# Three query heads ahead of the expert rows, five among them

## The reference

```
qh = (t @ w_q).reshape(T, 8, 2, 128)                 # queries: two halves for each of 8 heads
s = einsum('thpd,hpnd->thpn', qh, sub_keys)          # key scores: 128 for each half
s_top, i_top = top_k(s, 16)                          # the best 16 of each half
cand = s_top[:, :, 0, :, None] + s_top[:, :, 1, None, :]
best, pos = top_k(cand.reshape(T, 8, 256), 16)       # the best 16 pairs: 16 experts for a head
g = softmax(best)
act = gelu(einsum('thkd,td->thk', u_tab[idx], t))
out = einsum('thk,thkd->td', g * act, v_tab[idx])
```

## Time and profile before

| | |
|---|---|
| median of 3 runs | 1783.69 us (1779.28 to 1784.22) |
| the profiled execution | 1787.91 us |
| its span | 1786.0 us |
| busy: PE, DVE, ACT, POOL | 87%, 58%, 43%, 15% |
| DMA | 431.63 MB, mean 242 GB/s |
| of these the gathers (queue 0) | 268.45 MB |
| chain that ended last, by engine | PE 59%, DMA 25%, ACT 7%, DVE 6% |

### The profile page before, as it was taken

How to read it: one execution, slowest core, us unless ns; L and a number is a source line. 1 busy time by engine, 2 the same in 40 slices (tenths; PEclk the granted TensorE clock), 3 DMA queues, 4 the chain that set the end, 5 groups by cost and what they waited for, 6 DMA issues and landing times.

```text
span 1786.0 us, 22981 instructions
## 1 busy us (share of the span) xinstructions
PE 1553.8 (87%) x8461; PEld 1127.9 (63%) x8461; DVE 1030.4 (58%) x2060; ACT 763.5 (43%) x1628; POOL 268.5 (15%) x260
## 2 busy tenths in 40 slices
PE   8899999978888877887777769988999988889997
PEld 5699559864233322322222239878999986889997
DVE  3345326435666666766666456544676676466665
ACT  2444333215444444444444343443555545454553
POOL 0000000104334444444444300000000000000000
PEclk9899999989999999999999999968999997899999
DMA  7355544487999999999999944402555541235552
GB/s 249 121 169 183 165 165 131 154 305 293 420 414 419 421 420 419 420 420 420 419 419 421 420 158 139 145 1 93 191 188 179 177 131 55 72 118 188 179 176 91
DMA packets 175284, 431.63 MB, mean 242 GB/s; under 512 B 6764, under 2 KB 133345, under 8 KB 142305
## 3 DMA queue, kind: packets, MB, share of 16 engines
q0 software_dynamic: 36864, 268.45, 36.4%
q1 hardware_dynamic: 137178, 159.51, 27.5%
q10 hardware_dynamic: 1159, 2.58, 0.4%
HBM read 429.47 MB, written 1.05 MB: 241 GB/s over the span
## 4 chain that ended last, share of the span: by engine, by line
PE 59%; DMA 25%; ACT 7%; DVE 6%; issue 2%; POOL 0%; ACTq 0%; DVEq 0%; SPq 0%; POOLq 0%
PE banks L577 27%; DMA arena<-in_peer_uv,experts 16%; PE banks L926 8%; PE banks L1018 6%; PE banks L680 4%; DMA tok_a<-in_peer_uv,experts 3%; PE banks L610 3%; PE banks L809 2%; PE banks L783 2%; DMA tok_b<-in_peer_uv,experts 2%; PE banks L656 2%; DMA wring<-in_peer_w_q 1%; DVE wlow L1427 1%; PE banks L767 1%; ACT diag L1267 1%
## 5 line engine op out<-in xcount | busy, mean ns | idle before, releaser
L926 PE MATMUL banks<-arena,diag 128*128 128x512 f32 x824 | 403.0, 622 | 102.9 <-ACT diag L1267 102.8
L1427 DVE TENSOR_TENSOR wlow<-wring,whigh 128x1024 fp32r<-128x1024 f32 x234 | 275.9, 1222 | 214.3 <-ACT whigh L1050 214.2
L577 PE MATMUL banks<-a_high,whigh 128*128 128x256 f32 x1256 | 368.0, 293 | 28.8 <-DVE a_low L1435 21.9
L926 PEld LDWEIGHTS banks<-arena,diag 128*128 128x128 f32 x824 | 146.1, 192 | 355.2 <-ACT diag L1267 227.0
L577 PE MATMUL banks<-a_low,whigh 128*128 128x256 f32 x1256 | 361.2, 288 | 0.0
L577 PE MATMUL banks<-a_high,wlow 128*128 128x256 f32 x1256 | 360.8, 287 | 0.0
L1771 DVE CUSTOM_DVE_ANT_0 arena<-arena,scores 128x1024 f32<-128x1024 f32 x206 | 252.3, 1225 | 179.6 <-DMA arena<-in_peer_uv,experts 178.6
L1050 ACT ACTIVATE whigh<-wring 128x1024 fp32r<-128x1024 f32 x234 | 234.3, 1050 | 272.2 <-DMA wring<-in_w_up 110.3
L1381 POOL DMA_INDIRECT arena<-in_peer_uv,experts x206 | 216.3, 1050 | 688.7 <-DVE experts L1735 349.1
L577 PEld LDWEIGHTS banks<-a_high,whigh 128*128 128x128 f32 x1256 | 246.2, 196 | 34.5 <-issue 29.3
L577 PEld LDWEIGHTS banks<-a_low,whigh 128*128 128x128 f32 x1256 | 246.8, 197 | 2.6 <-issue 2.6
(11 more groups left out here) (214 smaller groups left out, 2055.8 us busy)
## 6 DMA issues: line engine op xcount, KB each, us to landing
wring<-in_w_up SPq DMA_DIRECT2D x44, 1024.0 KB, 5.2
wring<-in_w_mod SPq DMA_DIRECT2D x24, 1024.0 KB, 5.2
wring<-in_w_down SPq DMA_DIRECT2D x22, 1024.0 KB, 5.0
wring<-in_w_in SPq DMA_DIRECT2D x17, 1024.0 KB, 5.4
wring<-in_w_qkv_a SPq DMA_DIRECT2D x12, 1024.0 KB, 5.1
wring<-in_peer_w_q SPq DMA_DIRECT2D x8, 1024.0 KB, 5.8
wring<-in_w_mix_out SPq DMA_DIRECT2D x4, 1024.0 KB, 5.2
wring<-in_w_o_a SPq DMA_DIRECT2D x4, 1024.0 KB, 5.2
```

Of the source, the lines that this page charges most:

```text
L577: mm = nc.tensor.matmul(dst, l(k), r(k), start=first and n == 0, stop=last and n == 2)
L926: mm = nc.tensor.matmul(banks[:, 2 + 2 * b + half, :], diag[:, n % DIAGS, :], ring[n % RING][:, D + half * 512:D + (half + 1) * 512], star ...
L1427: V.tensor_tensor(low, w, high.bitcast(F32), ALU.subtract).then_inc(w_split, 1)
```

## The change

Only heads 0, 1 and 2 are made ahead of the rows. Each of the heads 3 to 7 is made inside the row loop: in the group of 16 rows h - 3 its first half of the columns comes on PE behind the second row of the group, the second half behind the sixth, the key scores behind the tenth; ACT's two copies stand behind the eighth and the twelfth row. The query product takes banks 0 and 1 in turn (four banks before). The order of the scores and the turns of `h2` with heads 1 and 2 is another: the scores of head 1 no longer stand behind head 2, and all four turns go with head 1. The four modulation chunks of the row loop move from rows 32, 48, 64 and 80 to rows 88, 96, 104 and 112 and use bank 6. The order in which SP loads chunks is the same. DVE's and POOL's programs are the same.

More of the change, by code:

```diff
@@ L674, in mod_chunk @@
                 started = i not in (0, MODS_1, MODS_2)
-                if started and mod_bank(i) == 7:
+                if started and mod_bank(i) == mod_bank(i - 1):
                     mod_turn(i - 1)
@@ L682, in mod_chunk @@
                 mm.then_inc(mod_rows, 1)
-                if started and mod_bank(i) != 7:
+                if started and mod_bank(i) != mod_bank(i - 1):
                     mod_turn(i - 1)
@@ L1232, in scores_out, with query_out @@
                 copy(head_sc[:, :, h, :], banks[:, 4 + h % 2, :].rearrange("p (b n) -> p b n", b=TB)).then_inc(ps_read, 1)
-            for h in range(PEER_HEADS):
+            def query_out(h):
                 act.wait_ge(pq_made, h + 1)
@@ L1237, in _, with h2_out @@
                     act.wait_ge(ps_made, h - 1)
[L1238 to L1246, removed]
+                copy(peer_q[:, h % 2, :, :].rearrange("p s t -> p (s t)"), banks[:, h % 2, :]).then_inc(pq_read, 1)
+            def h2_out(g):
+                act.wait_ge(h2_turned, g + 1)
+                copy(h2tok[:, g // 2, (g % 2) * 512:(g % 2 + 1) * 512], banks[:, 6 + g % 2, :]).then_inc(h2_read, 1)
+            for h in range(EARLY_HEADS):
[5 more added lines that the diff above has]
+                    h2_out(g)
             def weights_of(g):
```

## The result

| | before | after |
|---|---|---|
| median | 1782.84 us (1779.28 to 1784.22, 4 runs) | 1760.68 us (1757.63 to 1766.45, 4 runs) |
| ratio | | 0.9883, 95% interval 0.9851 to 0.9914 |
| the profiled execution, its span | 1787.91, 1786.0 us | 1757.63, 1755.7 us |
| busy PE, DVE, ACT, POOL in the span | 87%, 58%, 43%, 15% | 88%, 59%, 43%, 16% |

22 us faster; 19.2 were forecast (1764.5 us), and the range of 1757 to 1775 holds the median. A second set of runs gave 1761.73 us and 0.986 (0.9829 to 0.9891).

The account below looks back on a forecast made before the run. The row loop was taken as bound by the DMA wire; profiled 1787.9 us, less 20.5 idle wire, plus 1.3 thin start, gave 1768.7, and 4.2 lower for the median, 1764.5 us; range 1757 to 1775.

Parts of the forecast that it names:

- The wire bounds the rows: Row loop, 450 to 1023 us: 256 gathers of 1.05 MB at 419 GB/s, one row per 2.524 us, limited by DMA.
- The idle wire of 20.5 us: DMA idle time before the full stretch, 14.7 us up to 410.80 plus 5.8 us up to 425, by busy shares.
- Row 0 near 371, row 10 39.8 us earlier: PE begins row 0 near 371.0 instead of 410.81; row 10 is issued near 374.8 instead of 414.63.
- A thin start costs 1.3 us: Only two or three rows under way until about 390, against eight in the full stretch; 1.3 us off the gain.
- Five chunks at 3.1 us: Weights of heads 6 and 7 and three modulation chunks now travel inside the full stretch: 15.3 us off 34.4 us head start.
- the two methods: Gain estimated as head start less chunks, 19.1 us, and as idle wire less thin start, 19.2 us; within 0.1.
- The Trainium skill's rule on small descriptors: About three extra bus cycles per packet: a weight chunk costs an estimated 8% over a row, 2.7 us; five cost 13.7.
- PE, ACT and DVE hide their part; nobody waits for weights: Inside the rows, head work costs nothing further: PE has 5 us spare per group; loads come at least 24 rows early.
- A: Slower rival: ring length, not wire rate, bounds the rows, so PE work between rows adds whole; 1798 us, 5 in 100.
- C: No-change rival: row 0 starts later, near 390 on, behind a hidden ACT or DVE wait; 1781 us, 5 in 100.
- D: Larger-gain rival: idle wire counted in bytes, not busy shares, gives 24.4 us; 1759.5 us, 10 in 100.
- B: Thin-start rival: head 3's first half runs at lower clock, 6.9 us, leaving wire empty; gain 12, 1772 us, 15 in 100.

Follow-up runs that it names:

- pe_burden: Changed kernel plus twenty blocks of extra PE products on constants inside the rows, 69 us of PE time without transfers; 1761.9 us, ratio to before 0.9882.
- no_mods: Changed kernel without loading the last four modulation chunks, their products reusing head 7's query weights; 1750.78 us, ratio to before 0.9796.
- early5: Changed kernel with five heads made ahead of the rows instead of three, three inside them; 1760.51 us, ratio to before 0.9854.
- early6: Changed kernel with six heads made ahead of the rows instead of three, two inside them; 1778.53 us, ratio to before 0.9976.
- norm_first: Changed kernel with group 0's weights normalised behind row 0's dot product instead of row 4's; 1761.18 us, ratio to before 0.9871.
- ring8: Changed kernel with eight buffers instead of ten in the ring of gathered rows; 1766.51 us, ratio to before 0.99.
- no_loads: Changed kernel without loading the weights of heads 3 to 7, which reuse the chunks of heads 0 to 2; 1758.35 us, ratio to before 0.9857.

## Why the prediction was right, point by point

- *The wire bounds the rows:* shown, by pe_burden (69 us of PE work for nothing) and no_mods (four loads of 1.05 MB less, with the program of PE, DVE, ACT and POOL unchanged, and 11.5 to 12.3 us less).
- *The idle wire of 20.5 us is what can be won:* the stretch became 21.8 us shorter, 21.0 in the second execution. early5 shows that PE's work ahead of the rows does not count while the hole stays closed, early6 that it opens again.
- *Row 0 near 371, row 10 39.8 us earlier:* row 0 at 365.59, in a trace whose first gather is 5.2 us earlier; on the clock of before that is 370.8. Row 10 went out 25.3 us behind the first gather instead of 65.1: 39.8. The last gather went out at 996.44, or 1001.6 on the clock of before, 21.8 us earlier; near 1004 was forecast.
- *Row 4's landing sets row 0:* right (the earlier trace rows gave 13.0 us, now 12.7), though norm_first shows that it does not matter.
- *A thin start costs 1.3 us:* **this term was mis-sized.** After has no stretch under 1.00 there; the tenth row landed at 356.77 + 19.7 = 376.5, when rows 10 and 11 had been out since 369.64 and 371.94, and row 12 followed at 377.11. The thin start exists, but shows only when fewer bytes stand in front of it: 3.2 us in ring8, 0.6 by the share in no_loads, 2.5 in early6. Without the term the forecast is 20.5, against 21 to 22.
- *Five chunks at 3.1 us:* the price is right (no_mods), the number isn't. 34.4 - 15.3 = 19.1 comes out 1.9 to 2.7 us too low, and the trace of before shows why. The prediction counted five chunks as travelling behind the tenth row's landing, but the weights of heads 6 and 7 had been issued at 361.76 and 369.56 and went partly beside the ten rows. Between that landing and the start of row 10 (382.25 to 416.60 us) the queue of the weights moved 4.53 MB, or 4.3 chunks of 1.05 MB, as this line of the DMA view for that stretch has it (packets, MB, share):

```profile
q1 hardware_dynamic: 4503, 4.53, 40.6%
```

With 4.3 in place of five it is 34.4 - 4.3 x 3.1 = 21.1, against 21.0 and 21.8 measured. So the two methods agreed within 0.1 because each was low for a reason of its own, which was chance.
- *The Trainium skill's rule on small descriptors* ("DMA: Bandwidth & Descriptors", "Why small descriptors are slow (HBM only)") gave 2.7 us for a chunk as an estimate; no_mods measures 2.9 to 3.1, the row of before 3.1. So the trace again speaks for more.
- *PE, ACT and DVE hide their part; nobody waits for weights:* right. Among the waits between 350 and 1030 us there is none of PE for a transfer. ACT waits five times for a query product, 10.3 us in all, and the wire stays full over them.
- *Rivals:* A is refuted, C did not happen, D's 24.4 us are 2.6 above the larger of the two gains. B had two parts. The lower clock did not reach head 3: its first half took 3.45 us and not 6.9, at a granted clock of 1.00 from 371 to 381 us, and rows 12 and 13 were out at 377.11 and 378.86, not near 387. The thin start is real in ring8 and early6, and without effect here.
- *The median:* the forecast moved it from 1783.7 to 1764.5 and it came out 3.8 us lower. 1.3 of these are the thin start, 0.8 a median of before that stands at 1782.84 with its fourth run; the other 1.7 are within the runs' own 5 us. By whole runs alone 20.5 and 22 can't be told apart.

## What to carry to other kernels

Where a stage runs at the wire's rate, look for the idle time of the wire and not of the engines: work ahead of it is worth taking away only until the first buffers' transfers reach to the next issue, here the difference between six heads (18 us) and five (nothing). Past that point a shorter way to the first row gives nothing, more PE work in the rows costs nothing (up to 131 busy of 140 us here), and each transfer that falls into the full stretch costs its share of the wire. The next gain is then a transfer moved into an idle stretch, for which a buffer must be free, and a ring that can be made shorter may give it: 5 to 5.8 us in the stretch for two chunks here, though not clear of noise in whole runs.

## What the runs showed of the hardware

- A load of 1.05 MB in 1 KB packets costs the stream of 8 KB rows 2.9 to 3.1 us (no_mods), where a row of the same size takes 2.5 (before). It lands 26 us after its issue beside the gathers (26.5 before, 25.8 to 26.5 after) and 5.8 us after it alone (before). In the changed kernel nobody waited for one, with at least 24 rows between issue and use; in before, whose heads stand ahead of the rows, PE waited for one until 379.57.
- Eight rows of 1.05 MB in the ring are enough to keep the wire at 1.01 from 450 to 992 us, over PE interruptions of 3.45 us (ring8).
- Parts that a change does not touch moved by several microseconds from one execution to the next: the first gather's issue between 344.4 and 349.5 us in twelve of the thirteen profiled executions (360.3 in ring8), the part behind the rows from 731 to 742 us. The stretch between two marks around the change repeated to 0.8 us in the one pair that there is.
- Open: in after, ACT's copy of head 2's scores begins 2 us after PE's last product of them (353.69 us after, the scores beginning at 350.41). It had 7.4 us to spare, so it cost nothing; its cause wasn't looked for.
